# The opening of a two-layer decoder kernel reordered: transposes ahead of the parameters, first norm weights spread by matmuls, bias flips behind the third and fifth group

## The reference: what is computed

```python
for layer in range(DEPTH):
    h = rms_norm(x, norm_mix[layer])
    proj = h @ w_in[layer]
    (a_qkv, a_beta, a_alpha, a_gate, b_q, b_f, b_i, b_gate, c_qkv, br_gate) = jnp.split(proj, offsets, axis=-1)
    o_a = gated_deltanet(...)
    o_b = hgrn2(...)
    o_c = dilated_attention(c_qkv, qnorm_c[layer], knorm_c[layer], rel_bias)
    x = x + mix @ w_out[layer]
    h = rms_norm(x, norm_ffn[layer])
    x = x + swiglu(h, ffn_w1[li], ffn_w3[li], ffn_w2[li])   # even layers; experts in odd ones
```

## Time and profile before

| | |
|---|---|
| median of 3 executions | 2110.97 us (2110.39 to 2113.51) |
| profiled execution, its own time | 2111.69 us |
| its span in the profile | 2109.9 us |
| PE busy | 2024.1 us, 96% |
| PEld busy | 1728.0 us, 82% |
| DVE busy | 1609.2 us, 76% |
| ACT busy | 1232.6 us, 58% |
| read from memory | 513.86 MB, 245 GB/s over the span |

### The profile page before, as it was taken

The page is one execution under the profiler, slowest core; times in us unless marked ns, Lnnn a source line. Parts: engine busy times, 40 slices in busy tenths (PEclk is TensorE's granted clock), DMA queues, the critical chain, the costliest instruction groups (busy, mean ns, idle before and its releaser), DMA issues.

```text
span 2109.9 us, 28760 instructions
## 1 busy us (share of the span) xinstructions
PE 2024.1 (96%) x10759; PEld 1728.0 (82%) x10759; DVE 1609.2 (76%) x1256; ACT 1232.6 (58%) x1013; POOL 16.2 (1%) x22
## 2 busy tenths in 40 slices
PE   7999999989997999999979999999999999999997
PEld 6988888779997988888767888888788888888885
DVE  5878855755444878955766898898889889898986
ACT  4544455444333554455445777777677777777774
POOL 0000000000000000000000000000000000000000
PEclk9999999999999999999998999999999999999999
DMA  8523455245554532455346999999899999999995
GB/s 277 164 81 100 140 164 189 86 150 183 193 181 131 179 100 81 140 162 188 109 149 233 381 355 378 372 356 380 325 382 355 378 371 357 376 360 382 354 375 187
DMA packets 240500, 517.26 MB, mean 245 GB/s; under 512 B 11519, under 2 KB 34167, under 8 KB 240412
## 3 DMA queue, kind: packets, MB, share of 16 engines
q1 hardware_dynamic: 238124, 507.60, 67.9%
q0 software_dynamic: 2288, 8.41, 1.1%
HBM read 513.86 MB, written 2.12 MB: 245 GB/s over the span
## 4 chain that ended last, share of the span: by engine, by line
PE 89%; DVE 6%; ACT 2%; issue 2%; DMA 0%; SPq 0%; DVEq 0%; ACTq 0%
PE PS L478 26%; PE PS L480 25%; PE PS L479 25%; PE PS L549 7%; PE PS L1003 1%; DVE lo L1561 1%; ACT hi L1116 1%; PE PS L980 1%; PE PS L498 1%; PE PS L760 0%; DVE a_act L1662 0%; DMA rows<-in_knorm_c 0%; PE PS L950 0%; DVE t_n L1584 0%; PE PS L791 0%
## 5 line engine op out<-in xcount | busy, mean ns | idle before, releaser
L1561 DVE TENSOR_TENSOR lo<-raw,hi 128x2048 fp32r<-128x2048 f32 x481 | 1095.6, 2290 | 296.3 <-ACT hi L1116 293.9
L1116 ACT ACTIVATE hi<-raw 128x2048 fp32r<-128x2048 f32 x481 | 919.6, 1915 | 353.3 <-PE PS L480 344.9
L478 PE MATMUL PS<-hi,e_hi 128*128 128x512 f32 x896 | 356.3, 398 | 4.7 <-ACT hi L1116 3.3
L480 PE MATMUL PS<-hi,e_lo 128*128 128x512 f32 x896 | 350.5, 391 | 0.0
L479 PE MATMUL PS<-lo,e_hi 128*128 128x512 f32 x896 | 349.9, 391 | 0.0
L478 PE MATMUL PS<-hi,actT_hi 128*128 128x512 f32 x640 | 253.9, 397 | 4.6 <-DVE lo L1561 4.1
L480 PE MATMUL PS<-hi,actT_lo 128*128 128x512 f32 x640 | 249.6, 390 | 0.0
L479 PE MATMUL PS<-lo,actT_hi 128*128 128x512 f32 x640 | 249.1, 389 | 0.0
L478 PE MATMUL PS<-hi,fT_hi 128*128 128x512 f32 x536 | 208.8, 389 | 1.8 <-DVE fT_lo L1584 1.8
L480 PE MATMUL PS<-hi,fT_lo 128*128 128x512 f32 x536 | 208.7, 389 | 0.0
L479 PE MATMUL PS<-lo,fT_hi 128*128 128x512 f32 x536 | 208.7, 389 | 0.0
(11 more groups left out here) (323 smaller groups left out, 2154.8 us busy)
## 6 DMA issues: line engine op xcount, KB each, us to landing
raw<-in_moe_w SPq DMA_DIRECT2D x336, 1024.0 KB, 5.6
raw<-in_w_in SPq DMA_DIRECT2D x92, 1024.0 KB, 5.1
raw<-in_ffn_w SPq DMA_DIRECT2D x33, 1024.0 KB, 5.3
raw<-in_w_br SPq DMA_DIRECT2D x12, 1024.0 KB, 5.0
raw<-in_w_out SPq DMA_DIRECT2D x8, 1024.0 KB, 5.0
hankel<-hankel_dram POOLq DMA_DIRECT2D x1, 1536.0 KB, 13.5
x<-in_x SPq DMA_DIRECT2D x2, 512.0 KB, 3.7
gain<-in_norm_mix POOLq DMA_DIRECT2D x2, 512.0 KB, 6.1
```

Source lines behind the costliest of these rows:

```text
L478: pe.matmul(out, a_hi, b_hi, start=first, stop=False, skip_group_check=True)
L480: return pe.matmul(out, a_lo, b_hi, start=False, stop=last, skip_group_check=True)
L1116: act.activation(hi[prog.u % SPLIT][:, :], raw[slot][:, :], COPY).then_inc(hi_made.sem, 1)
L1561: dve.tensor_tensor(lo[prog.u % RAW][:, :], raw[prog.u % RAW][:, :], hi[s][:, :].bitcast(F32), ALU.subtract).then_inc(lo_made.sem, 1)
```

## The change

**SP** now loads one row of norm weights (into partition 0 of `gain`), the identity alone, `x`, the first two weight units, `ab` and `a_par`, then the other masks, then the rest. **ACT** issues the loads of `picks`, `table` and `rows`, before its own work. **POOL** no longer loads the first norm weights. **PE** begins with 22 float32 matmuls of 128x128 ones by ones, which nothing reads, then spreads the row of norm weights over 128 partitions of two PSUM banks (two matmuls with one row of weights each), and DVE's first norm reads the weights from there. PE transposes `hn` next, then does the parameters' matmuls, and eight more of ones by ones. `turn_input` no longer ends in the wait for all of `actT_lo`: in both layers' mixers the first half of the first group waits for two pieces of it, then runs ahead of the narrow product, which moves from bank 5 to bank 7; the dense and the experts' blocks wait as before, one line later. DVE and ACT do the parameters behind the first unit. The bias flips move behind the third and the fifth group, into banks 4, 5, 6 and then 5, 6, 7. `ids_here` is folded into `slots_here`.

```diff
-            pe.wait_ge(actT_lo_made.sem, actT_lo_made.at(L, idx + 3))
...
-        def group_T(pair):
-
-            for half in range(2):
+        def group_T(pair, halves=(0, 1), hold=False):
+
+            for half in halves:
                 w_hi, w_lo = unit_ready()
                 for ct in range(4):
+                    if hold and ct == 2:
+                        pe.wait_ge(params_kept.sem, 2)
...
-        pe.wait_ge(consts_here.sem, 32)
-        pe.wait_ge(rows_here.sem, 16 * N_ROW_LOADS)
-        pe.transpose(PS[:, 0, 0:R_N], rows[0:R_N, :], ident[0:R_N, 0:R_N]).then_inc(rows_T.sem, 1)
...
+        pe.wait_ge(tiny_made.sem, 5)
+        for _ in range(22):
+            mm(PS[:, 7, 0:P], ones, ones)
+
+        pe.wait_ge(first_here.sem, 32)
+        for half in range(2):
+            ins = mm(PS[:, half, :], ones_t[0:1, :], gain[0:1, half * 512:(half + 1) * 512])
+        ins.then_inc(params_done.sem, 1)
+
+        def parameters():
+
+            pe.wait_ge(picks_here.sem, 16)
+            pe.wait_ge(table_here.sem, 17)
+            for g in range(GROUPS):
+                ins = pe.matmul(PS[0:H, 1 + g, 0:DIST], table[:, g * H:(g + 1) * H], picks[:, g, :],
+                                start=True, stop=True)
+            ins.then_inc(params_done.sem, 1)
+            pe.wait_ge(rows_here.sem, 16 * N_ROW_LOADS)
+            pe.transpose(PS[:, 3, DIST:DIST + R_N], rows[0:R_N, :], ident[0:R_N, 0:R_N]).then_inc(params_done.sem, 1)
+            for _ in range(8):
+                mm(PS[:, 0, 0:P], ones, ones)
...
-                mm(PS[:, 4 + n % 3, :], consts[:, K_FLIP, :],
+                mm(PS[:, 4 + n % 3 + n // 3, :], consts[:, K_FLIP, :],
...
         def mixer(L):
...
             turn_input(lambda t, k: hn[:, t, k * P:(k + 1) * P], 0, L)
+            if L == 0:
+                parameters()
+            pe.wait_ge(actT_lo_made.sem, actT_lo_made.at(L, 1))
+            group_T(0, (0,), hold=L == 0)
+            pe.wait_ge(actT_lo_made.sem, actT_lo_made.at(L, 3))
             pe.wait_ge(ab_split.sem, 2)
-            narrow_product(5, L)
...
+            narrow_product(7, L)
+            group_T(0, (1,))
+            if L == 0:
+                pe.wait_ge(params_kept.sem, 2)
+            turn_narrow(4, L).then_inc(ab_done.sem, 1)
+            group_T(1)
+            pe.wait_ge(a_raw.sem, a_raw.at(L, 1))
+            group_T(0)
+            if L == 0:
+                pe.wait_ge(masks_here.sem, 16)
+                spread_bias(0)
...
             group_T(0)
+            if L == 0:
+                spread_bias(3)
...
@@ ACT, mixer @@
             prep(2)
             conv_in(1)
-            bias_copies(L, 0)
             conv_tanh(0)
             prep(2)
             conv_in(2)
-            bias_copies(L, 3)
             conv_tanh(1)
-            prep(2)
+            prep(1)
+            bias_copies(L, 0)
+            prep(1)
...
@@ DVE, norm @@
-            dst, g = (fn, f_gain) if phase else (hn, gain)
+            dst, g = (fn, f_gain[:, :]) if phase else (hn, gain[:, :])
+            if L == 0 and phase == 0:
+                g = PS[:, 0:2, :].rearrange("p a b -> p (a b)")
...
@@ SP @@
+        load(gain[0:1, :], dram["norm_mix"][0:1, :], first_here)
+        load(consts[:, K_ID, :], dram["masks"][:, K_ID, :], first_here)
         for t in range(TT):
-            load(x[:, t, :], xr[t], x_here)
...
+            load(x[:, t, :], xr[t], x_here[t])
+        cols(0, C_QKV)
```

More of the change, by code:

```diff
@@ L287, in build @@
     dve_step = signal("dve_step")
-    x_here = signal("x_here")
-    consts_here = signal("consts_here")
+    x_here = [signal(f"x_here{t}") for t in range(TT)]
+    first_here = signal("first_here")
+    masks_here = signal("masks_here")
+    picks_here = signal("picks_here")
     rows_here = signal("rows_here")
@@ L1135, in norm_scale @@
             load_tables()
-            if L == 0 and phase == 0:
-                act.wait_ge(x_here.sem, 32)
-            else:
+            if L or phase:
                 act.wait_ge(x_made.sem, x_made.at(L if phase else L - 1, 1 if phase else 2))
@@ L1146, in norm_scale, with load, split_narrow, parameters @@
             act.activation(stat[:, 4:6], stat[:, 2:4], EXP, scale=-0.5).then_inc(norm_r.sem, 1)
+        def load(dst, src, sig):
+            act.dma_start(dst, src).then_inc(sig.sem, 16)
+        load(picks[:, :, :], dram["buckets"], picks_here)
+        load(table[0:BUCKETS, :], dram["rel_bias"], table_here)
+        rows_of_small = (
+            (R_CONV, dram["conv_a"].rearrange("l t (c p) -> (l t c) p", p=P)),
+            (R_LB, dram["lb_logits"].rearrange("l (h p) -> (l h) p", p=P)),
+            (R_GA, dram["gnorm_a"]), (R_GB, dram["gnorm_b"]),
+            (R_QN, dram["qnorm_c"].rearrange("l g p -> (l g) p")),
+            (R_KN, dram["knorm_c"].rearrange("l g p -> (l g) p")))
+        assert len(rows_of_small) == N_ROW_LOADS
+        for r, src in rows_of_small:
+            load(rows[r:r + src.shape[0], :], src, rows_here)
         act.wait_ge(tiny_made.sem, 4)
         norm_scale(0, 0)
[L1151 to L1161 removed]
+        def split_narrow():
+            act.wait_ge(ab_here.sem, 48)
+            act.activation(ab_hi[:, :, :, :], ab[:, :, :, :], COPY).then_inc(ab_split.sem, 1)
+        def parameters():
+            act.wait_ge(params_done.sem, 3)
+            act.activation(by_dist[:, :, :], PS[0:H, 1:1 + GROUPS, 0:DIST], COPY).then_inc(params_kept.sem, 1)
+            act.activation(small[:, :], PS[:, 3, DIST:DIST + R_N], COPY).then_inc(params_kept.sem, 1)
+            act.wait_ge(par_here.sem, 32)
+            act.activation(a_rate[:, :, :], a_par[:, 0, :, :], EXP).then_inc(a_rate_e.sem, 1)
         def turn_input(idx, L, scale=1.0):
@@ L1592, in _ @@
             dve.memset(tiny[:, n:n + 1], v).then_inc(tiny_made.sem, 1)
-        dve.memset(ones_t[:, :], 1.0).then_inc(dve_step.sem, 1)
-        dve.wait_ge(dve_step.sem, prog.step())
+        dve.memset(ones_t[:, :], 1.0).then_inc(tiny_made.sem, 1)
         dve.memset(table[BUCKETS:BUCKETS + 1, :], 1.0).then_inc(table_here.sem, 1)
@@ L1642, in mixer @@
                 prep(1)
+            if L == 0:
+                prep(1)
             turn_input(0, L)
             if L == 0:
-                prep(3)
+                prep(1)
+                split_narrow()
+                prep(1)
             dve.memset(a_in[:, :, 0:3], 0.0).then_inc(pad_made.sem, 1)
             dve.wait_ge(pad_made.sem, L + 1)
+            if L == 0:
+                parameters()
+                dve.wait_ge(masks_here.sem, 16)
             def conv(g):
@@ L2331, in _ @@
                  .rearrange("q o l h -> q (o l) h"), par_here)
+        load(consts[:, K_ID + 1:K_N, :], dram["masks"][:, K_ID + 1:K_N, :], masks_here)
         def mixer(L):
-            for g in range(3):
+            for g in range(0 if L else 1, 3):
                 cols(L, C_QKV + g * W)
```

142 lines of the change are left out of this document (59 added, 83 removed).

## The result

| | us |
|---|---|
| before, median of 14 runs beside the changed kernel (range) | 2111.99 (2108.75 to 2114.89) |
| changed, median of 14 runs (range) | 2115.09 (2111.74 to 2121.69) |
| ratio, 95% interval | 1.0018 [1.001, 1.0026] |
| profiled execution, its span, mean granted clock | 2113.70, 2111.9, 0.984 |

The account below looks back on a forecast made before the run. PE bounds the kernel (89% of the chain). First group's end from 36.81 to 35.9 us (-0.9) plus layer 1 (-1.35) gave -2.25: 2109.4 on the profiled execution, 2108.7 us as median; range 2105.8 to 2113.0.

Parts of the forecast that it names:

- I take the clock as fallen in the idle time and back when the transposes end, as layer 1 had it.: Opening: after 2.6 us idle, transposes run at 1.2 GHz, then parameters and eight ones at 2.4; first wide matmul at 21.7.
- rival B: Opening: clock stays low through transposes, parameters and ones; first group ends at 41.0, total 2113.8 us; chance 0.19.
- The ones matmuls: PE's start: 22 products from 1.9 us, clock rising at 7.0, done at 9.7.
- Layer 1: Layer 1's opening: first half of the first group starts without waiting for the fourth piece of `actT_lo`; 1.35 us gained.
- The opening's terms: Opening: ones to 9.7, spreading 1.7 us to 11.4, DVE's norm 2.48, transposes from 14.0; row factors by 9.5, hidden.
- Rival A: Opening: clock stays up through the 2.6 us idle; group ends at 34.1, total 2106.0 to 2106.9 us; chance 0.22.
- C: Opening: ones matmuls never raise the clock; first group ends about 45.4, total 2118.2 us; chance 0.07.
- D: Third group: moved bias flips uncover DVE, PE waits 1 us for its unit; total 2109.7 us; chance 0.08.
- The Trainium skill's rule: Opening: transposes don't count as PE activity, so would never raise the clock; the prediction held the trace disagreed.

Follow-up runs that it names:

- f2: Changed kernel with 127 instructions of padding ahead of layer 1's norm, 256 with its own 129: 2114.16 us, ratio 1.0018.
- g4: Changed kernel without the 8 ones products behind the parameters, padded in two places to 256 instructions: 2114.82 us, ratio 1.001.
- f1: Kernel before with 129 instructions of waits that do nothing, in PE's idle time in layer 1: 2113.22 us, ratio 1.0015.
- f4: Kernel before with 40 instructions of waits that do nothing, in PE's idle time in layer 1: 2113.69 us, ratio 1.0018.
- g1: Changed kernel with 10 more ones products behind the spreading, without the 8 behind the parameters, padded to 256 instructions: 2106.51 us, ratio 0.9981.
- g2: g1 without its 119 instructions of padding: 2109.59 us, ratio 0.9991.
- h3: g1 with the bias flips where the kernel before has them: ratio 0.9987.
- e1: Changed kernel measured again with no edit: 2117.7 us, ratio 1.0031.
- f3: Changed kernel with 10 more ones products behind the spreading and 44 instead of 22 at the front: 2117.47 us, ratio 1.004.
- e5: Changed kernel with 10 more ones products behind the spreading, filling PE's idle time before the transposes: 2119.11 us, ratio 1.004.
- h4: g1 unchanged, measured again: 2108.41 us, ratio 0.9986.

## Why the prediction was wrong, point by point

- **"I take the clock as fallen in the idle time and back when the transposes end, as layer 1 had it."** This step failed. It turned one profile into one path, and set rival B beside it as an alternative with a chance of 0.19. Half of the changed kernel's runs lie 5.8 us above the others (median 2118.12 against 2112.33). Its two profiles, of the lower half, went by the forecast; two profiles with the same opening up to the transposes (f2, g4) show B. That the upper half is B is the best reading, not shown by a profile of it.
- **The code, a term put at nothing.** "The ones matmuls" were priced by their time on PE, 9.7 us, all of it covered. Their 120 instructions (each product is two weight loads and two matmuls) were not priced as code. They moved the experts' loop over a block's edge: 1.7 to 1.9 us seen at the third pass, 3.1 to 3.7 us by the medians of three pairs (before with f1 and f4, g1 with g2), 2.1 to 3.8 by their ratios. No rival had it. The rest lies at the kernel's end: behind the last `hi` copy the seven profiles with fetches in the third pass took 0.6 to 2.0 us more than before's, the eleven without from 0.1 less to 0.7 more. From 2086 to 2096 us before had a clock of 1.00, the changed kernel 0.83, with a fall of 3.4 us that stands in five of the seven and in none of the eleven. Why isn't settled.
- **Layer 1** was gained as forecast (1.24 us of 1.35 in the changed profile), but the prediction had it kept to the end. The experts' opening took 1.3 us back there, and 0.5 to 2.3 us in every other profile with the split.
- **B's price.** Its end of the first group was forecast at 41.0 and came at 39.4, so the opening was priced too high, but the prediction let the lag stay constant behind it. In f2 it was 2.6 us behind before at the first group's end and 5.0 at the experts' door, since other low stretches lengthened too.
- **The opening's terms** were right within 0.6 us. The ones took 8.12 us, not 7.8, and the spreading 1.98, not 1.7, so the transposes began at 14.60, not 14.0. `x` came late too (the row factors at 10.33, bound 9.5), but under the spreading.
- **Rival A's** path came true only where the idle time was filled. Its argument misread rows 7 and 8: 9.30 us is the whole idle time, and the clock was already at 0.52 in the us from 652, 2.6 us after PE's last matmul. The idle time here is as long as that, not far shorter.
- **C** is refuted: the clock rose during the ones in all twelve profiles that have them, at 5.0 to 8.1 us. **D** is refuted by the changed profile: ACT's 5th and 21st `hi` copies, on either side of the moved flips, start 0.34 and 0.35 us ahead of before's. h3's time agrees, within its noise.
- The Trainium skill's rule cited with B, that transposes don't count for the clock, again isn't borne out: it rose at 18.3, with transposes on PE from 14.60 to 18.0. B came all the same, so a right argument against the rule was no argument against B.

Against before's median the forecast was -2.25 us; the changed kernel's lower group measured +0.3, all its runs +3.1. The fetches (2.1 to 3.8) and layer 1's gain taken back (1.3) would put the lower group 1.2 to 2.9 us above before. It stood 0.3 above it here and 3.5 in e1, the same kernel measured again, so the account holds only roughly. The upper group explains why all runs together lie higher.

## What to carry to other kernels

Filler work on PE costs code as well as time: before adding a hundred instructions ahead of a loop that almost fills PE's instruction buffer, count where the loop begins and ends in 16 KB blocks, compare the instruction queue's packets pass by pass, and pad to a whole block if they grew, in idle time long enough for the padding. Where a plan rests on the clock being back by a certain instruction, take it as a draw and not as a path, look at the mean clock of all runs for two groups, and close the idle gap itself rather than warm up on both sides of it; then look whether thin matmuls (few rows of weights) lie in the filled stretch, since the clock fell behind such ones in f3. Follow a gain to the kernel's end before booking it: layer 1's was gone 430 us later. A single profile of the good sort can look just like the forecast while half of the executions do something else.

## What the runs showed of the hardware

- **PE keeps a loop of seven blocks.** From 1715 to 1960 us a pass of 1766 instructions ran without a packet in eleven profiles. The section of the Trainium skill cited above calls the buffer a FIFO of only two lines, in a remark beside the sizes; by that every pass would be fetched, and here the measurement decides against it. The pass of seven blocks agrees with the 128 KiB for PE that the same section states. The second pass is fetched in every kernel, before's too, with nine packets.
- **The clock's changes don't stand still against the program.** The same 22 products from 1.83 us took 8.12, 8.09, 6.76 and 6.68 us in four executions (changed, e5, f2, g1), in which the level rose at 8.1, 8.0, 5.2 and 5.0.
- **The same kernel waits 1.6 us more or less at the second pass's start.** Here g1 and h4, which are one file:

```profile
1478.27 0.47 PE L477 MATMUL PS<-hi,e_hi 128*128 128x512 f32 x1 [1.53 <-DVE lo L1612]
```
```profile
1476.09 0.68 PE L477 MATMUL PS<-hi,e_hi 128*128 128x512 f32 x1 [3.14 <-ACT hi L1142]
```

  The longer wait is in before's profile as well (3.30 us); of the 18 profiles, nine have the longer wait, eight the shorter, and e5 both a short and a long one.
